# Routed experts' down product: activations as the stationary operand, sums by token, transposed back once a stage

## The reference, cut to what matters

```python
def hier_moe(xn, w_group, b_group, w_expert, b_expert, w_gate, w_up, w_down):
...
    cw = jnp.einsum('tk,tke->te', comb, jax.nn.one_hot(expert_id, N_EXPERTS, dtype=jnp.float32)).astype(xt.dtype)
    hid = jax.nn.silu(jnp.einsum('td,edf->tef', xt, w_gate)) * jnp.einsum('td,edf->tef', xt, w_up)
    y = jnp.einsum('tef,efd->td', hid * cw[:, :, None], w_down)
    return y.reshape(b, s, d)
```

## Time and profile before

| | |
|---|---|
| median of three runs | 3963.59 us (3963.14 to 3971.35) |
| profiled execution | 3968.26 us, of which 3966.3 us lie between its first and last instruction (the span) |
| mean granted clock of TensorE | 0.972 of 2.4 GHz |
| matmul busy, weight loads busy | 3727.6 us (94%), 3462.0 us (87%) |
| VectorE, ScalarE, GpSimd busy | 2674.1 us (67%), 1738.8 us (44%), 743.7 us (19%) |
| matmul records | 28914 |
| down products (TensorE reads `ex` and `wp`) | 5856 records, 285 ns mean, 748.0 us busy |
| chain that ended last, shares of the span | PE 68%, DVE 21%, ACT 7%, issue 2%, POOL 1% |

### The profile page before, as it was taken

How to read it: one execution, slowest core, us unless ns; L and a number is a source line. 1 busy time by engine, 2 the same in 40 slices (tenths; PEclk the granted TensorE clock), 3 DMA queues, 4 the chain that set the end, 5 groups by cost and what they waited for, 6 DMA issues and landing times.

```text
span 3966.3 us, 68495 instructions
## 1 busy us (share of the span) xinstructions
PE 3727.6 (94%) x28914; PEld 3462.0 (87%) x28914; DVE 2674.1 (67%) x4778; ACT 1738.8 (44%) x2951; POOL 743.7 (19%) x555
## 2 busy tenths in 40 slices
PE   7999999999999889989999989999999998889899
PEld 7779998799989767789998969999979998777799
DVE  4567876688677665567777776777667765665554
ACT  3353344533454443344545644444454544433343
POOL 2024442244300421110002420000100002322100
PEclk9899999999999899999999999999999999999999
DMA  5126753277567310057674416767437663300142
GB/s 208 70 80 242 270 197 123 92 275 266 195 246 267 104 70 1 1 192 273 237 273 162 146 54 236 271 232 276 154 128 273 236 258 132 101 17 1 63 177 107
DMA packets 64113, 664.83 MB, mean 168 GB/s; under 512 B 7104, under 2 KB 7616, under 8 KB 8512
## 3 DMA queue, kind: packets, MB, share of 16 engines
q1 hardware_dynamic: 63808, 660.46, 44.6%
HBM read 659.38 MB, written 1.05 MB: 167 GB/s over the span
## 4 chain that ended last, share of the span: by engine, by line
PE 68%; DVE 21%; ACT 7%; issue 2%; POOL 1%; DMA 0%; SPq 0%; DVEq 0%; ACTq 0%; POOLq 0%
PE pb L273 66%; DVE wp L226 6%; DVE ring L243 4%; ACT wp L264 3%; DVE sq L226 2%; PE pb L280 2%; DVE wk L238 2%; DVE wk L226 2%; DVE sq L238 1%; ACT sq L264 1%; DVE hT L238 1%; ACT wk L264 1%; DVE rsb L226 1%; ACT ex L264 1%; POOL sq L226 0%
## 5 line engine op out<-in xcount | busy, mean ns | idle before, releaser
L273 PE MATMUL pb<-hx,wp 128*128 128x256 f32 x15360 | 1935.0, 286 | 77.7 <-DVE hx L238 37.6
L273 PEld LDWEIGHTS pb<-hx,wp 128*128 128x128 f32 x15360 | 1892.9, 194 | 99.4 <-issue 78.2
L226 DVE TENSOR_TENSOR wp<-ring,wp 128x1024 fp32r<-128x1024 f32 (+1 forms) x847 | 1021.3, 1240 | 351.7 <-ACT wp L264 350.9
L264 ACT ACTIVATE wp<-ring 128x1024 fp32r<-128x1024 f32 x936 | 937.8, 1046 | 212.0 <-PE pb L273 207.8
L226 POOL TENSOR_TENSOR wp<-ring,wp 128x512 fp32r<-128x512 f32 (+1 forms) x243 | 484.2, 2006 | 1610.4 <-ACT wp L264 1568.8
L273 PE MATMUL pb<-ex,wp 128*128 128x256 f32 x5856 | 748.0, 285 | 20.0 <-DVE ex L226 17.5
L273 PEld LDWEIGHTS pb<-ex,wp 128*128 128x128 f32 x5856 | 723.7, 193 | 25.5 <-DVE ex L226 17.9
L243 DVE CUSTOM_DVE_ANT_0 ring<-ring,cact,prm 128x1024 f32<-128x1024 f32 x288 | 418.6, 1501 | 0.0
L273 PE MATMUL pb<-wk 128*128 128x128 f32 (+8 forms) x3008 | 388.3, 293 | 22.0 <-ACT wk L264 6.9
L273 PEld LDWEIGHTS pb<-wk 128*128 128x128 f32 (+4 forms) x3008 | 286.3, 172 | 115.8 <-issue 45.4
L264 ACT ACTIVATE sq<-pb 128x256 f32<-128x256 f32 (+1 forms) x216 | 88.4, 409 | 669.6 <-PE pb L273 600.0
(11 more groups left out here) (186 smaller groups left out, 2709.3 us busy)
## 6 DMA issues: line engine op xcount, KB each, us to landing
ring<-weights SPq DMA_DIRECT2D x385, 1536.0 KB, 6.7
ring<-weights SPq DMA_DIRECT2D x41, 1024.0 KB, 4.9
ring<-weights SPq DMA_DIRECT2D x4, 512.0 KB, 9.6
cst<-consts SPq DMA_DIRECT2D x1, 2032.0 KB, 10.6
ring<-weights SPq DMA_DIRECT2D x1, 1280.0 KB, 5.5
ring<-weights SPq DMA_DIRECT2D x1, 1152.0 KB, 5.0
xT<-xT_in SPq DMA_DIRECT2D x1, 1024.0 KB, 4.8
xT_out<-xT SPq DMA_DIRECT2D x1, 1024.0 KB, 3.9
```

The lines of the kernel that those rows point to most:

```text
L226: return self.real.tensor_tensor(out, a, b, op) if self.real else Uncounted()
L264: return self.real.activation(out, a, func, bias=bias, scale=scale, accum_out=accum)
L273: return self.real.matmul(out, l, r, start=start, stop=stop, skip_group_check=skip)
```

## The change

Down products of routed stages (where `cw` is given) swap their operands: the hidden activations are the stationary operand, 128 tokens at a time, and the down weights the moving one, 512 columns at a time. A unit has 4 sums of 128 tokens x 512 features, one bank each, and 12 matmuls where it had 24. Behind the last unit ScalarE copies the four banks to `hT` by token; TensorE turns the 1024 features back with 16 transposes of 128x128 into banks 4 to 7 (`turn_back`); VectorE's eight adds then read these. Feed-forwards keep their order and operands. The signal for a finished down product, which ScalarE and VectorE wait for three units later, is now raised once a unit.

```diff
+    def by_token(t, a, b):
+        return hT[:, t * 1024 + a:t * 1024 + b]
...
+            else:
+                for hf in range(2):
+                    for t in range(2):
+                        if u == 0:
+                            bk.hold(e, 2 * hf + t, (st, "y", hf, t), (a_out, (st, "y", hf, t)))
+                        ins = mm3(e, pb[2 * hf + t][:, :], [a[:, t * 128:(t + 1) * 128] for a in (eh[u % 3], el[u % 3])],
+                                  [a[:, hf * 512:(hf + 1) * 512] for a in (p.hi, p.lo)], u == 0, u == g.units - 1)
+                        over = [("used", p.at), (st, "down", u)] if hf and t else []
+                        over += [(st, "y", hf, t)] if u == g.units - 1 else []
+                        if over:
+                            ins.then_inc(*product.up(*over))
+
+        def turn_back():
             for m in range(8):
...
+                if m % 2 == 0:
+                    ps = bk.hold(e, 4 + m // 2, (st, "yT", m // 2), (x_new, (st, m + 1)))
+                for t in range(2):
+                    e.wait_ge(*a_out[st, "y", m // 4, t])
+                    ins = e.tp(ps[:, (m % 2) * T + t * 128:(m % 2) * T + (t + 1) * 128],
+                               by_token(t, m * 128, (m + 1) * 128))
+                ins.then_inc(*turned.up((st, "yT", m)))
...
         down(g.units - 1)
+        if cw is not None:
+            turn_back()
         bk.use(range(8))
...
             silu(u)
             high(u)
+        for hf in range(2 if cw else 0):
+            for t in range(2):
+                e.wait_ge(*product[st, "y", hf, t])
+                e.act(by_token(t, hf * 512, (hf + 1) * 512), pb[2 * hf + t][:, :], ACT.Copy).then_inc(
+                    *a_out.up((st, "y", hf, t)))
...
         for m in range(8):
-            e.wait_ge(*product[st, "down", g.units - 1, m | 1])
-            finish(m, pb[m // 2][:, (m % 2) * T:(m % 2 + 1) * T])
+            e.wait_ge(*(turned if cw else product)[st, "yT", m | 1])
+            finish(m, pb[(4 if cw else 0) + m // 2][:, (m % 2) * T:(m % 2 + 1) * T])
```

More of the change, by code:

```diff
@@ L924, in down @@
             e.wait_ge(*x_lo[st, "hid", u])
-            for m in range(8):
[L926 to L932, removed]
+            if cw is None:
+                for m in range(8):
+                    if u == 0 and m % 2 == 0:
+                        bk.hold(e, m // 2, (st, "y", m // 2), (x_new, (st, m + 1)))
+                    ins = mm3(e, pb[m // 2][:, (m % 2) * T:(m % 2 + 1) * T], part((p.hi, p.lo), m * 128),
+                              (eh[u % 3], el[u % 3]), u == 0 and m % 2 == 0, u == g.units - 1)
+                    if m % 2:
+                        over = [("used", p.at), (st, "down", u)] if m == 7 else []
+                        ins.then_inc(*product.up((st, "yT", m), *over))
+            else:
[10 more added lines that the diff above has]
+        def turn_back():
+            for m in range(8):
+                if m % 2 == 0:
[5 more added lines that the diff above has]
+                ins.then_inc(*turned.up((st, "yT", m)))
         for u in range(g.units):
@@ L961, in silu @@
                 if u >= 3:
-                    e.wait_ge(*product[st, "down", u - 3, 7])
+                    e.wait_ge(*product[st, "down", u - 3])
                 e.act(sg[u % 3], bank(st, "glu", u)[:, 0:T], ACT.Silu).then_inc(*a_out.up((st, "silu", u)))
```

## The result

After the change the median is 3972.05 us (3969.86 to 3977.47, 20 runs); the kernel before, run beside it, has 3965.64 (3963.01 to 3973.07, 20 runs). The ratio is 1.0015 with a 95% interval of 1.0008 to 1.0022, that is +5.9 us (3.2 to 8.7). So the change is a loss: small, clear of the noise, and under the 0.2% that the prediction drew as its line for no change.

The account below looks back on a forecast made before the run. The prediction took the loop of VectorE and ScalarE, 17.89 us per two routed units, as the bound. Stage ends of +4.21 and +3.65 less 0.2 gave +7.7 us on 3963.59, so 3971.3 us, range 3965.5 to 3977.

Parts of the forecast that it names:

- The loop: Steady part of routed stages: VectorE and ScalarE set the pace, 17.89 us per two units, so the change gains nothing there.
- growing waits on TensorE: Sign in the steady part: TensorE's wait before down products grows from 0.33 us per two units to some 0.7.
- Rounds shorter than 17.8 us: Sign in the routed units that the forecast is wrong in kind: TensorE then had a say in the pace.
- The price of the matmul: Down products of routed units: a matmul of 512 columns taken at 0.225 us, between about 0.21 and 0.24.
- the cover: Steady part: the VectorE and ScalarE round of 17.89 us hides TensorE's matmuls, unless one costs over 0.254 us.
- the rival that TensorE sets the pace: Routed units: TensorE is the bound, -20.5 us at best, -12.8 with the stage's end, so 3950.8 us; chance 0.07.
- The start of the stage: First down products: ScalarE's split goes 0.2 us earlier, GpSimd still sets VectorE's end; counted 0, at most 0.35 gained per stage.
- The end of the stage: Copy, table load, squares, pair sums and mean in series: mean 6.64 us after the last down product, +4.21 and +3.65 us.
- D itself: D is the end of a routed stage's last down product; forecast to come about 0.1 us earlier (0 to 0.32).
- The sum: Both stage ends together: 4.21 + 3.65 - 0.2 = +7.7 us; chance of the forecast as summed 0.50.
- The shorter tail: Rival at the stage's end: squares and table load overlap, adds set the end, +4.7 us, 3968.3 us; chance 0.10.
- The lowered clock: Rival at the stage's end: mean's matmuls at half clock level, +8.7 to +10 us in all, 3972.3 to 3973.6; chance 0.28.

Follow-up runs that it names:

- e1: The changed kernel without the copies to hT and the transposes at the stage's end, wide matmuls kept, output not the reference's: 3967.26 us, ratio 1.0002 to the kernel before.
- e3: The kernel before with the routed stages' adaptive-norm sums on VectorE cut from 1024 to 32 columns, output not the reference's: 3937.81 us, ratio 0.9924.
- e4: The changed kernel with the routed stages' adaptive-norm sums cut from 1024 to 32 columns: 3936.68 us, ratio 0.9922 to the kernel before.
- e2: The changed kernel with the next norm's table load issued ahead of the four copies in the routed stages: 3972.03 us, ratio 1.0010 to the kernel before.
- e5: The kernel before with ScalarE's high split of the first weight piece made one unit earlier in routed stages, nothing left out: 3947.62 us, ratio 0.9948.

## Why the prediction came out right

**The loop.** Right, and shown three times: the round of 17.88 us unchanged with the chain round VectorE and ScalarE, e1 at the time of before, and e3, in which nothing but VectorE's work is cut, 30 us faster. The expected sign of growing waits on TensorE was there: the weight loads wait 0.58 us ahead of one down product in two (480.62) where it was 0.33, for a predicted 0.7. One sign was drawn too coarsely. Rounds shorter than 17.8 us were to mean that TensorE had a say, and TensorE's list has them in the first half of stage 1, 17.27 after and 17.50 before; VectorE's round is 17.88 there all the same, and the stretch from 320 to 560 us, which the prediction took as steady, was read from its second half.

**The price of the matmul.** 0.229 us measured for 0.225 taken, in the middle of the bounds 0.21 to 0.24. It made no difference under the cover, which ends at 0.254; where the cover is gone (e4) it is what decides, 0.113 us per unit. The 2.56 us a unit that the prediction gives as the best case is a little under what its row gives, 12 x 0.217 = 2.60, so the rival that TensorE sets the pace was priced at -20.5 us for some -18.

**The start of the stage.** Counted 0, and it is 0, by the way that was named. The first three down products end earlier, and ScalarE's split goes 3.05 us behind the first of them where it was 3.17 (timeline after, start of stage 1):

```profile
308.02 8.45 PE L273 MATMUL pb<-wp,ex 128*128 128x512 f32 x36 [1.27 <-DVE ex L226]
...
311.07 2.96 ACT L264 ACTIVATE wp<-ring 128x1024 fp32r<-128x1024 f32 x3 [2.32 <-PE pb L273]
...
316.76 0.41 DVE L226 TENSOR_TENSOR sq<-pb,rsb 128x256 f32<-128x256 f32 x1
```

VectorE's gate in the timeline of the kernel before:

```profile
314.30 0.41 DVE L226 TENSOR_TENSOR sq<-pb,rsb 128x256 f32<-128x256 f32 x1
```

But the gate comes 316.76 - 308.02 = 8.74 us behind, where it was 314.30 - 305.57 = 8.73. The 0.12 us are gone at the pieces beside GpSimd, where VectorE's two splits take 4.67 us for 4.55.

**The end of the stage.** The terms hold one by one: copy 0.60 as taken; the load ends at D + 1.93 (D + 1.94); two squares end at D + 2.68 (2.70); three pair sums end at D + 4.85 (4.99); the mean is read 1.66 behind them (1.65). The sum is 6.51 for a predicted 6.64, and the only term off is the pair sum, 0.70 for 0.75. The Trainium skill (ScalarE: Activation LUTs, What ACT_TABLE_LOAD costs) adds a drain to a load; the squares at 583.05 begin 0.02 us after the load of 581.75 + 1.28, so by the trace there is none here either.

**D itself.** This is the term of the sum that was mis-sized. The forecast was that D comes 0.1 us earlier in each stage (0 to 0.32). From the first down product it is -0.09 in stage 1 (581.10 - 308.02 = 273.08, before 273.17) and +1.08 in stage 4 (274.20, before 273.12). The lower level, 0.50, lay over part of the last down product in stage 1 (the stretch from 578.10 holds its end) and over all of it in stage 4 (the stretch from 1059.40), which then takes 5.46 us where it took 4.39. The argument that a half-clock stretch costs both kernels the same columns holds only if the stretch falls on the same place. It doesn't: the last down product took 4.33 and 5.46 in after, 4.58 and 5.46 in e1, 4.40 and 3.00 in e2, with the same idle 3.7 us ahead of it each time. The granted clock over it was 0.50 where it took 5.46 and 1.00 where it took 3.00.

**The sum.** For the profiled execution +3.99 + 4.60 = 8.6 us, predicted 7.7: -0.3 for the tails, +1.2 for D. The median rose by 6.4, the ratio says 5.9 (3.2 to 8.7). That the predicted 3971.3 lies so near 3972.05 is partly chance, since the median of before was taken as 3963.59 from three runs and is 3965.64 over twenty.

**The rivals.** TensorE as the bound fell with e1 and e3. The shorter tail fell with the timeline. The lowered clock was real as a mechanism, but it did not strike the mean in the profile after (1.00 over it, the stretch from 584.70); it struck the last down product instead, and the mean in e4.

## What to carry to other kernels

An engine that is busy 97% but that no chain and no wait names need not be the bound: before its work is cut, cut the other engine's in one run (e3) and see whether it takes the chain. A layout that shortens each turn of a loop and must be turned back behind it pays only where that engine is the bound and the saving per turn times the turns exceeds the serial end (here 28 x 0.113 = 3.2 against 2.5 to 3.5 us). When work is put in front of another stage, look at what that stage begins with: the table load came onto the path without a line of the diff touching it.

## What the runs showed of the hardware

- A matmul of 512 columns steps every 0.229 us, 36 in a row as well ((8.45 - 0.406) / 35 = 0.230), against 2 x 0.12 for two of 256. So 256 more columns cost 0.109 us, and an instruction some 0.011 beside its columns (an estimate, from a straight line through the two widths); the 0.217 us of 256 columns at the lower level, halved, give 0.108 for the columns and agree. Those 0.011 us are all that doubling the width saves.
- A VectorE instruction that reads two tiles of SBUF, started while GpSimd works on a piece, got its work done only when GpSimd's ended. It shows best in e3, where the first of three equal products of 32 columns takes ten times as long as the second (timeline):

```profile
458.08 4.19 POOL L226 TENSOR_TENSOR wp<-ring,wp 128x512 fp32r<-128x512 f32 x2 [4.55 <-ACT wp L264]
459.94 2.39 DVE L243 CUSTOM_DVE_ANT_0 ring<-ring,cact,prm 128x32 f32<-128x32 f32 x1
...
462.26 0.24 DVE L243 CUSTOM_DVE_ANT_0 ring<-ring,cact,prm 128x32 f32<-128x32 f32 x1
```

  The first ends at 459.94 + 2.39 = 462.33, GpSimd at 458.08 + 4.19 = 462.27. In the round of before the same is the 3.35 us of a product that takes 1.20 to 1.28 alone, some 2.1 us in each 17.89. VectorE's gate, which reads PSUM and one tile of SBUF, isn't held: in e5 it takes its usual 0.42 us at 456.99, amid GpSimd's 454.25 to 458.78. The Trainium skill (GPSIMD Engine Reference, 1. Specifications) says that GpSimd shares its SBUF interfaces with VectorE, with contention for instructions of two SBUF inputs; the trace agrees, and here the price was nearly the whole rest of GpSimd's instruction.
- The same idle 3.7 us ahead of the last down product was followed by 3.00 to 5.46 us for it: where the lower level falls at a stage's end differs from one profile to the next, by up to 2.5 us, as much as the largest terms of the sum.
